# Dense attentions: scores two pairs ahead in front of the values, head squares on GpSimd

## The reference, cut to what matters

```
# layer 0, differential attention: a pair of maps is one head of 128 value columns
s = q_blk @ k.T + bias            # 2 maps per head, causal: -inf above the diagonal
p = softmax(s, axis=-1)
a = p[:, :, 0] - lam * p[:, :, 1]
o = a @ v
o = o * rsqrt(mean(o * o, axis=-1) + LN_EPS)      # over each head's 128 columns
o = o * subln_g * (1.0 - lam_init)
# layer 1, block attention; with 256 tokens there is one block, so it is causal softmax
p = softmax(q_c @ k_own.T * scale + b_own); o = p @ v_own
```

## Time and profile before

| | us |
|---|---|
| median of 3 runs | 2344.18 (2343.15 to 2344.76) |
| span of the profiled execution | 2343.1 |
| first attention, turn_p of pair 2 to finish of pair 7 | 97.88 to 126.84 |
| second attention, turn_p of pair 1 to finish of pair 7 | 433.24 to 463.35 |

### The profile page before, as it was taken

The page is one execution under the profiler, slowest core; times in us unless marked ns, Lnnn a source line. Parts: engine busy times, 40 slices in busy tenths (PEclk is TensorE's granted clock), DMA queues, the critical chain, the costliest instruction groups (busy, mean ns, idle before and its releaser), DMA issues.

```text
span 2343.1 us, 24410 instructions
## 1 busy us (share of the span) xinstructions
PE 2071.3 (88%) x7378; PEld 1194.7 (51%) x7378; DVE 1424.3 (61%) x2979; ACT 876.4 (37%) x2140; POOL 1003.6 (43%) x1080
## 2 busy tenths in 40 slices
PE   7889999899999988798978999896999998778776
PEld 6668887678868643453433443342445443223222
DVE  3574555464566579874576664476846548684445
ACT  4544544554534432662223252223335223222222
POOL 0100000100000047677567556656755756777774
PEclk9999999999999999999999999998999999999998
DMA  8425545245535679999999999999999999999997
GB/s 307 176 90 180 196 161 198 72 153 179 190 133 197 246 318 409 348 398 412 414 410 408 416 408 413 411 414 394 405 417 406 413 412 386 411 409 410 409 409 309
DMA packets 172555, 752.62 MB, mean 321 GB/s; under 512 B 19184, under 2 KB 19472, under 8 KB 152864
## 3 DMA queue, kind: packets, MB, share of 16 engines
q0 software_dynamic: 148640, 544.05, 58.6%
q1 hardware_dynamic: 22224, 198.37, 22.6%
q10 hardware_dynamic: 1584, 8.91, 1.0%
HBM read 750.18 MB, written 4.22 MB: 322 GB/s over the span
## 4 chain that ended last, share of the span: by engine, by line
PE 47%; DMA 21%; DVE 13%; POOL 8%; issue 8%; ACT 2%; DVEq 1%; POOLq 0%; SPq 0%; ACTq 0%
PE ps L999 12%; DMA Z<-u,experts 10%; DMA Z<-v,experts 9%; PE ps L730 8%; PE ps L731 8%; PE ps L732 8%; DVE Z L2064 5%; PE ps L1019 5%; POOL Z L2420 4%; POOL Z L2435 3%; POOL ring L2435 1%; DMA ring<-panels 1%; DMA ring<-v,experts 1%; PE ps L1076 1%; DVE ring_lo L1875 1%
## 5 line engine op out<-in xcount | busy, mean ns | idle before, releaser
L999 PE MATMUL ps<-Z 128*128 128x512 f32 x1792 | 850.7, 620 | 159.7 <-DMA Z<-v,experts 96.6
L2064 DVE CUSTOM_DVE_ANT_0 Z<-Z,ps 128x1024 f32<-128x1024 f32 x512 | 612.1, 1219 | 410.7 <-DMA Z<-u,experts 404.5
L999 PEld LDWEIGHTS ps<-Z 128*128 128x128 f32 x1792 | 335.6, 196 | 633.9 <-issue 393.1
L2420 POOL DMA_INDIRECT Z<-u,experts x512 | 487.8, 953 | 284.5 <-issue 135.5
L2435 POOL DMA_INDIRECT Z<-v,experts x448 | 427.8, 955 | 261.7 <-PE ps L999 152.8
L1875 DVE TENSOR_TENSOR ring_lo<-ring,ring_hi 128x1024 fp32r<-128x1024 f32 x212 | 247.9, 1221 | 195.2 <-ACT ring_hi L1312 194.9
L1488 ACT ACTIVATE hdot<-hdot 128x4 f32<-128x4 f32 x128 | 26.3, 205 | 655.9 <-DVE hdot L2064 655.8
L730 PE MATMUL ps<-ring_hi,xT_lo 128*128 128x512 f32 x592 | 237.7, 402 | 14.4 <-DVE xT_lo L1934 9.2
L1019 PE MATMUL ps<-ring,o 128*128 128x512 f32 x528 | 232.3, 593 | 2.0 <-issue 2.0
L731 PE MATMUL ps<-ring_lo,xT 128*128 128x512 f32 x592 | 232.5, 393 | 0.0
L732 PE MATMUL ps<-ring_hi,xT 128*128 128x512 f32 x592 | 232.5, 393 | 0.0
(11 more groups left out here) (285 smaller groups left out, 2146.5 us busy)
## 6 DMA issues: line engine op xcount, KB each, us to landing
ring<-panels SPq DMA_DIRECT2D x106, 1024.0 KB, 5.0
ring<-panels SPq DMA_DIRECT2D x37, 2048.0 KB, 10.4
Z<-u,experts POOLq DMA_INDIRECT x512, 13.0
Z<-v,experts POOLq DMA_INDIRECT x448, 13.3
Z<-panels SPq DMA_DIRECT2D x3, 2048.0 KB, 22.5
gain<-gains ACTq DMA_DIRECT2D x4, 1024.0 KB, 4.8
bias_lines<-bias_line POOLq DMA_DIRECT2D x1, 3072.0 KB, 13.8
gain<-gains ACTq DMA_DIRECT2D x5, 512.0 KB, 6.7
```

Of the source, the lines that this page charges most:

```text
L999: last = mm(ps[:, c, :], diag[s], vrow[s][:, c * NC:(c + 1) * NC], start=slot == 0, stop=slot == SLOTS - 1 or n == SUMMED[-1] - 1)
L2064: v.tensor_tensor_reduce(out=row, in0=row, in1=dotted, scale=1.0, scalar=0.0, op0=ALU.mult, op1=ALU.add, accum_out=hdot[:, t, slot:slot + 1])\
L2420: g.indirect_dma_start(out=urow[s], out_offset=None, in_=(u0, u1)[layer], in_offset=bass.IndirectOffsetOnAxis(ap=experts[:, t, slot:slot + ...
```

## The change

On PE, scores(p+2) go in front of values(p) and turn_qk(p+3) behind them; turn_qk(2) stands in front of the loop. On ACT, exps(p+1) come right behind evict_pt(p), and evict_qk(p+3) behind them; the squares are gone. On DVE, soften(p+2) goes in front of finish(p). POOL stages a pair once the transposes of pair p-2 are done (it waited for their scores), and in the first attention squares the finished head p-3 behind the staging of pair p, into a buffer of six pairs. DVE sums all six pairs' squares with one reduction in front of the last finish. All loops over pairs are written out.

```diff
-        squares = Z[:, Z_WORDS - TILES * P:]
+        squares = Z[:, Z_WORDS - TILES * (PAIRS - 2) * P:].rearrange("p (t n d) -> p t n d", t=TILES, n=PAIRS - 2)
...
                 def run(self):                       # PE
+                    self.turn_qk(1, 0)
                     pe.wait_ge(s_read, self.base + AHEAD + 2)
-                    with pe.Fori(0, PAIRS // 2 - 1) as i:
-                        for u in range(2):
-                            self.turn_p(i, u)
-                            self.turn_qk(i + 1, u)
-                            self.values(i, u)
-                            self.scores(i + 1, u)
-                    for u in range(2):
-                        self.turn_p(PAIRS // 2 - 1, u)
-                        self.values(PAIRS // 2 - 1, u)
+                    for p in range(PAIRS):
+                        self.turn_p(p // 2, p % 2)
+                        if p + 2 < PAIRS:
+                            self.scores(p // 2 + 1, p % 2)
+                        self.values(p // 2, p % 2)
+                        if p + 3 < PAIRS:
+                            self.turn_qk((p + 3) // 2, (p + 3) % 2)
...
-                def sum_squares(self, p):            # ACT
-                    act.wait_ge(o_read, self.base + p + (AHEAD + 1))
-                    for t in range(TILES):
-                        last = f(squares[:, t * P:(t + 1) * P], o[:, t, p * P:(p + 1) * P], ACT.Square,
-                                 accum_out=stat[:, PAIRS * t + p:PAIRS * t + p + 1])
-                    last.then_inc(head_sums, 1)
...
                 def run(self):                       # ACT
-                    if self.base == 0:
-                        for p in range(PAIRS - 2):
-                            self.evict_pt(p // 2, p % 2)
-                            self.evict_qk(p // 2 + 1, p % 2)
-                            self.exps((p + 1) // 2, 1 - p % 2)
-                            self.sum_squares(p)
-                    else:
-                        with act.Fori(0, PAIRS // 2 - 1) as i:
...
+                    self.evict_qk(1, 0)
+                    for p in range(PAIRS):
+                        self.evict_pt(p // 2, p % 2)
+                        if p + 1 < PAIRS:
+                            self.exps((p + 1) // 2, (p + 1) % 2)
+                        if p + 3 < PAIRS:
+                            self.evict_qk((p + 3) // 2, (p + 3) % 2)
...
+                def sum_squares():                   # DVE
+
+                    dve.wait_ge(squared, PAIRS - 2)
+                    v.tensor_reduce(over(stat[:, 0:1], [[PAIRS, TILES], [1, PAIRS - 2]]), squares, AX.X, ALU.add)
+
                 soften(0, 0, FIRST_SCORES[0])
                 soften(0, 1, FIRST_SCORES[1])
-                if kind == "diff":
-                    for p in range(PAIRS - 2):
-                        finish(p // 2, p % 2)
+                for p in range(PAIRS):
+                    if p + 2 < PAIRS:
                         soften(p // 2 + 1, p % 2)
...
+                    if kind == "diff" and p == PAIRS - 1:
+                        sum_squares()
+                    finish(p // 2, p % 2)
...
                 elif step == "heads":
                     dve.drain()
-                    dve.wait_ge(head_sums, PAIRS - 2)
...
-                with pool.Fori(0, PAIRS // 2) as i:  # POOL
-                    for u in range(2):
-                        p = i * 2 + (base + u)
-
-                        apart(pool, (s_done, p + (AHEAD - 1)))
...
+                for p in range(PAIRS):
+                    u, at = p % 2, p * P
+
+                    pool.wait_ge(qk_done, base + p + (AHEAD - 1))
+                    g.tensor_copy(stage[u][:, :, 0, :], pj[:, :, at:at + P])
+                    last = g.tensor_copy(stage[u][:, :, 1, :], pj[:, :, D + at:D + at + P])
+                    last.then_inc(staged, 1)
+                    if kind == "diff" and 3 <= p:
+                        square_heads(p - 3)
+                if kind == "diff":
+                    square_heads(PAIRS - 3)
+
+            def square_heads(p):
+
+                pool.wait_ge(o_read, p + (AHEAD + 1))
+                g.tensor_tensor(squares[:, :, p, :], o[:, :, p * P:(p + 1) * P], o[:, :, p * P:(p + 1) * P], ALU.mult)\
+                    .then_inc(squared, 1)
```

More of the change, by code:

```diff
@@ L508, in build @@
         squares_ready = sem("squares_ready")
-        head_sums = sem("head_sums")
+        squared = sem("squared")
         root_ready = sem("root_ready")
@@ L1415, in evict_pt @@
                     copy(PT[u], ps[:, 4:6, 0:S_COLS]).then_inc(pt_ready, 1)
-                def sum_squares(self, p):
-                    act.wait_ge(o_read, self.base + p + (AHEAD + 1))
-                    for t in range(TILES):
-                        last = f(squares[:, t * P:(t + 1) * P], o[:, t, p * P:(p + 1) * P], ACT.Square,
-                                 accum_out=stat[:, PAIRS * t + p:PAIRS * t + p + 1])
-                    last.then_inc(head_sums, 1)
-                def run(self):
-                    if self.base == 0:
-                        for p in range(PAIRS - 2):
-                            self.evict_pt(p // 2, p % 2)
-                            self.evict_qk(p // 2 + 1, p % 2)
-                            self.exps((p + 1) // 2, 1 - p % 2)
-                            self.sum_squares(p)
-                    else:
-                        with act.Fori(0, PAIRS // 2 - 1) as i:
-                            for u in range(2):
[L1434 to L1440, removed]
+                def run(self):
+                    self.evict_qk(1, 0)
[5 more added lines that the diff above has]
+                            self.evict_qk((p + 3) // 2, (p + 3) % 2)
             def mlp(layer):
@@ L2399, in stage_pairs @@
                 pool.wait_ge(panel_used, 2 * (FIRST[f"in{call}"] + WIDTH[f"in{call}"] - 1))
-                with pool.Fori(0, PAIRS // 2) as i:
-                    for u in range(2):
-                        p = i * 2 + (base + u)
-                        apart(pool, (s_done, p + (AHEAD - 1)))
-                        g.tensor_copy(stage[u][:, :, 0, :], pj[:, :, bass.ds(i * (2 * P) + u * P, P)])
-                        last = g.tensor_copy(stage[u][:, :, 1, :], pj[:, :, bass.ds(i * (2 * P) + (D + u * P), P)])
-                        last.then_inc(staged, 1)
+                for p in range(PAIRS):
[12 more added lines that the diff above has]
+                    .then_inc(squared, 1)
             def gather_u(n):
```

## The result

The changed kernel takes 2330.78 us (median of 4 runs, 2330.19 to 2333.23), the kernel before 2344.27 beside it (4 runs, 2343.15 to 2344.76): the ratio over the runs is 0.9938, with an interval of 0.9926 to 0.9949. The two medians are 13.5 us apart (a ratio of 0.9942), where 10.9 were forecast: the mechanism held, and the gain came out a quarter larger than its terms. The profiled spans are 2343.1 and 2328.7.

A forecast was written before the change was run, and what follows sets the result against it. Rings of waits, not a full engine, clock or data, bound both attention loops. First attention 0.35 + 5.55 + 0.92 = 6.82, second 0.35 + 2.95 + 0.77 = 4.07, together 10.9: 2333.3 us, range 2330.7 to 2338.3.

The forecast's parts named there:

- the best end of the sum: Both attentions with every term at its favourable end: 13.2 us saved, or 2331.0.
- the squares' ring: First attention before the change: squares, evict_pt, values, finish, next squares set the 5.13 period; moving squares off ACT opens it.
- the rivals: Dear hand-overs, 2338.5, chance 0.14; gain waited for elsewhere, 2344.2, chance 0.07; GpSimd's square too slow, 2351.0, chance 0.05.
- this surcharge: First attention: with rings of 3.85, 3.92 and 3.87 a pair, the period was taken as 4.0, between 3.8 and 4.3.
- the GpSimd ring: First attention, over two pairs: turn_qk 0.48, turn_p 0.72, scores to soften, soften, finish, square, two staging copies; 3.87 a pair.
- the ring of exps: First attention, over two pairs: scores to soften 1.21, soften 2.05, finish 1.81, exps to turn_p 2.05, turn_p 0.72; 3.92 a pair.
- PE's ring: Both attentions: turn_p to evict_pt 0.94, to values 0.90, values 1.53, turn_qk 0.48; 3.85 a pair, between 3.75 and 4.17.
- The first pairs: Start of each attention: gains less than other pairs, turn_qk and evict_qk of pair 2 standing in front; 0.35 each, up to 0.55.
- The last pairs: End of each attention, turn_p(6) to finish(7): 8.51 to 7.59 saves 0.92 in the first, 7.92 to 7.15 saves 0.77 in the second.
- The reduction of 1.72: DVE's one reduction of 1536 values before finish(7), first attention: 1.72 long, of which 0.44 shows.
- Square 0.67: GpSimd's two-input square of a finished head, first attention: taken as 0.67, between 0.40 and 1.33.
- All of it moves forward: Stages behind each attention start when its last finish is done and find their weights there, so the whole saving carries through.

The follow-up runs named there:

- e11: The changed kernel run a third time, unaltered; 380.58 us from the second attention's end to the experts' first gather, no median given.
- e5: The changed kernel without GpSimd's squares and DVE's reduction, zeros in place of the sums for pairs 0 to 5; 2332.06 us, ratio 0.9936 to the kernel before.
- e7: The changed kernel with each GpSimd square one pair later, behind the staging of the pair four on; 2330.16 us, ratio 0.9929 to the kernel before.
- e6: The changed kernel with each GpSimd square done twice; 2336.37 us, ratio 0.9947 to the kernel before.
- e9: The changed kernel with squares one pair later, turn_qk before scores in the second attention only, and the reduction in two parts; 2329.55 us, ratio 0.9932.
- e1: The kernel before with only its loops over pairs written out, orders and squares as before; 2344.23 us, ratio 0.9989.
- e4: The changed kernel again, unaltered, beside other runs; 2331.43 us, ratio 0.9937 to the kernel before.

## Why the prediction came out short

The forecast was 2333.3 and the time 2330.78. That lies below the best end of the sum, 2331.0, and on the very edge of the stated range, 2330.7; by the ratio, 0.9938 of 2344.18, it would be 2329.6, below the range. The change did what was said of it: the squares' ring opened, scores went in front of values at no cost (turn_p to values takes 1.84 in the first attention and 1.85 in the second, and 0.94 + 0.90 was taken), and none of the rivals came. Where 10.9 were forecast the attentions gave 12.95. The steps that failed are sizes of terms, by 0.39 + 0.74 + 0.72 + 0.22 = 2.07, and one ring that was not named:

- *"When rings that share members are that close, each is now and then the late one; I take 4.0"*: this surcharge failed. The measured period is 3.92, five times 0.08 or 0.39 us less in all. The turn_p rows do alternate, 3.72, 4.04 and 3.74 (e11: 97.29, 101.01, 105.05, 108.79), but the sum of two is the GpSimd ring's 7.76, with nothing on top: 3.88, where that ring was worked out as 3.87. That the mean of five equals the 3.92 of the ring of exps is chance: it comes from the first pair's 4.09, and without the squares in the way the pairs take 3.81 to 3.82 (e5, e7), so that the ring of exps was put too long (scores to soften takes 1.07 for 1.21, soften 1.97 for 2.05). The 3.87 is luck in part, too: turn_qk to scores takes 1.46 with evict_qk in it, where 0.48 + 0.72 was taken, and shorter terms behind it make up for that. That the rings lie close together was right, as e5 and e6 show from both sides.
- *"In the second only PE's ring is left: 3.85":* it is 3.73 in the steady pair, because values take 1.44 (the estimate's low end was 1.45, and I took the old 1.53) and turn_qk to turn_p 0.44, not 0.48. It was not the only ring left either: the one through evict_qk, 3.72, was missing. Its mark is PE's 0.17 of waiting in front of scores, with evict_qk named, and no wait in front of values, where the prediction looked for 0.1 to 0.3. The fifth period has no turn_qk any more (there is no pair 8) and takes 3.61, which the prediction overlooked: (4 x 3.73 + 3.61) / 5 = 3.70, 5 x 0.15 = 0.74.
- *The first pairs, 0.35 each:* turn_p(0) to turn_p(1) fell from 4.56 to 3.69 in the first attention and from 4.41 to 3.68 in the second. What was put in front, turn_qk(2) and evict_qk(2), cost 0.1 there (scores to turn_p(0) 5.29 before, 5.38 after): turn_qk(2) starts at 88.97, beside the last of exps(0) (88.78 to 89.28), which turn_p(0) waits for in any order. So 0.78 and 0.64 were gained, more than the upper end of 0.55: in the second attention nearly what every other pair gains (0.74), in the first two thirds of it (1.19). That is 0.72 short in all.
- *The last pairs:* 8.51 to 7.43 and 7.92 to 7.09 saved 1.08 and 0.83 for 0.92 and 0.77, 0.22 short. The reduction of 1.72 (1.75), its place behind finish(6), and that part of it would show, were right; the part is 0.24 (turn_p(7) to finish(7) 3.69, and 3.45 in e9), not 0.44.
- *Square 0.67:* 0.61, with no share in the sum.
- *"All of it moves forward":* right. 295.5 us lie between the attentions in before, 295.3 in the changed kernel. Behind the second attention the profiles differ by more than that, and their clocks differ too. The 13.5 of the medians is the attentions' 12.95 and 0.5 that I cannot place.

## What to carry to other kernels

In a loop over four engines, list every chain that comes back to its own start, over one pair and over two; here the period was the longest of them, with nothing added for near ties. An edit that opens one ring is worth the distance to the next, so that edits must be costed together. Lengthening a member of a ring proves it, and removing it shows how far the next one is; compare the steady pairs alone, since a mean with the first pair in it hid both here. When an engine in the loop is full (DVE, 3.75 of 3.81), what it needs next goes first in every other queue.

## What the runs showed of the hardware

- **Staging and finish collide.** In the order of time of the kernel before, GpSimd's second staging copy (L2406) starts behind DVE's difference (L1837) and takes 0.59, where the first one takes 0.40:

```profile
98.45 0.45 DVE L1837 TENSOR_TENSOR o<-Z 128x256 f32<-128x256 f32 x1
...
98.56 0.59 POOL L2406 COPY Z<-pj 128x256 f32 x1
```

  In e1 the copy came first and the difference took 0.60, where it takes 0.42 in the changed kernel and 0.45 in the kernel before. In the changed kernel staging waits for the transposes instead, and the square for the difference itself: neither is slowed (copies 0.40, difference 0.42). The Trainium skill ("SBUF — State Buffer", section "Who interferes with whom") says that a DVE operation with two SBUF inputs and a GpSimd operation that reads SBUF exclude each other, the later one waiting; the rows agree in both orders that the later one is the longer, by 0.19 and 0.15 to 0.18, while the earlier one still had 0.34 and 0.33 to run. How long the later one stood still inside its time they don't show.
- **One kernel's executions differ by 1 us, and their clocks with them.** Of the changed kernel's three profiles two have the clock at 0.83 at 50 to 60 us and start the first scores at 84.14 and 84.13; in the third it is 1.00 there, and they start at 82.99. The table by stretch, of the changed kernel and of e4:

```profile
50.00:60.00 10.00, 8.38 (x30) 6.84 (x31) 4.72 (x4) 4.69 (x7) 2.18 (x4) 0.83 1.01 390
```

```profile
50.00:60.00 10.00, 8.36 (x35) 6.60 (x36) 5.27 (x5) 5.72 (x8) 1.68 (x4) 1.00 1.01 393
```

PE's busy time is the same (8.38 and 8.36) for 30 and 35 matmuls, and so is the kernel: what made the clock differ is not shown.
